# Cross attention's values product: four full-precision products a head become twelve on high and low parts

## The reference, cut to what matters

```
kv = mem @ mem_w_kv                      # once; 256 x 2048
mem_k, mem_v = split into 4 heads of 256
for each of the 2 layers:
    ...
    q = (x @ wq)                          # 256 x 1024, 4 heads of 256
    s = q @ mem_k.T / 16                  # each head, 256 x 256
    p = softmax(s)
    o = p @ mem_v                         # each head, 256 x 256: the changed product
    x = layer_norm(ALPHA * x + o @ wo)
    x = layer_norm(ALPHA * x + mlp(x))
```

## Time and profile before

| | |
|---|---|
| median of 3 runs | 953.45 us (952.93 to 953.58) |
| profiled execution, first to last instruction | 1903.2 us |
| PE busy in it | 1896.1 us |
| DVE busy | 710.1 us |
| ACT busy | 520.2 us |
| granted TensorE clock in it | 1.000 |

### The profile page before, as it was taken

One profiled execution on the slowest core, in us unless ns is written; L12 is line 12 of the kernel. 1 busy time (PEld: TensorE's weight loads), 2 busy tenths in 40 slices (PEclk: granted clock), 3 DMA queues, 4 the chain that ended last, 5 costly groups with the idle time before them and its releaser, 6 DMA issues.

```text
span 1903.2 us, 13114 instructions
## 1 busy us (share of the span) xinstructions
PE 1896.1 (100%) x5108; PEld 1373.0 (72%) x5108; DVE 710.1 (37%) x963; ACT 520.2 (27%) x732; POOL 60.6 (3%) x96
## 2 busy tenths in 40 slices
PE   9999999999999999999999999999999999999998
PEld 9669766766777776767666777667887667777766
DVE  6323234425343332443343343334334442232232
ACT  4233221313222223122132222232233232222221
POOL 0000000000000001000000000001000000000010
DMA  7332142215434433032154344341310243223200
GB/s 261 132 103 74 66 143 89 74 59 176 146 133 137 150 133 111 1 145 76 50 174 151 133 144 137 129 147 50 111 67 22 89 136 96 89 89 110 89 22 22
DMA packets 109660, 203.00 MB, mean 107 GB/s; under 512 B 4332, under 2 KB 75264, under 8 KB 106272
## 3 DMA queue, kind: packets, MB, share of 16 engines
q1 hardware_dynamic: 106000, 189.15, 29.7%
q0 software_dynamic: 3168, 12.24, 1.8%
q10 hardware_dynamic: 432, 0.79, 0.1%
HBM read 201.09 MB, written 1.06 MB: 106 GB/s over the span
## 4 chain that ended last, share of the span: by engine, by line
PE 99%; issue 0%; ACT 0%; DVE 0%; POOLq 0%; POOL 0%; ACTq 0%
PE WB L377 20%; PE YB L402 12%; PE YB L395 12%; PE YB L410 12%; PE WB L380 10%; PE YB L463 6%; PE WB L395 3%; PE WB L410 3%; PE WB L402 3%; PE WB L359 2%; PE WB L366 2%; PE WB L362 2%; PE YB L879 2%; PE WB L745 2%; PE WB L501 1%; PE YB L852 1%
## 5 line engine op out<-in xcount | busy, mean ns | idle before, releaser
L1801 DVE TENSOR_TENSOR wl<-raw,wh 128x2048 fp32r<-128x2048 f32 x144 | 331.5, 2306 | 283.4 <-ACT wh L1161 279.5
L377 PE MATMUL WB<-XS,wh 128*128 128x512 f32 x832 | 410.8, 675 | 0.0
L377 PEld LDWEIGHTS WB<-XS,wh 128*128 128x128 f32 x832 | 245.3, 303 | 118.0 <-issue 107.4
L1161 ACT CAST wh<-raw 128x2048 fp32r<-128x2048 f32 (+1 forms) x147 | 278.6, 1898 | 156.7 <-PE YB L410 84.3
L380 PEld LDWEIGHTS WB<-XS,wl 128*128 128x128 f32 x832 | 211.3, 317 | 35.3 <-issue 32.4
L380 PE MATMUL WB<-XS,wl 128*128 128x256 f32 x832 | 215.9, 440 | 0.0
L402 PE MATMUL YB<-wl,FHT 128*128 128x512 f32 x344 | 196.5, 676 | 0.0
L410 PE MATMUL YB<-wh,FLT 128*128 128x512 f32 x344 | 196.3, 674 | 0.0
L395 PE MATMUL YB<-wh,FHT 128*128 128x512 f32 x344 | 196.2, 673 | 0.0
L1343 ACT COPY U<-WB 128x256 f32<-128x256 f32 x102 | 33.0, 375 | 411.9 <-PE WB L380 411.9
L410 PEld LDWEIGHTS YB<-wh,FLT 128*128 128x128 f32 x344 | 103.1, 300 | 57.5 <-issue 49.5
(11 more groups left out here) (373 smaller groups left out, 1803.2 us busy)
## 6 DMA issues: line engine op xcount, KB each, us to landing
raw<-in_mlp_w SPq DMA_DIRECT2D x64, 1024.0 KB, 5.2
raw<-in_w_ada_t SPq DMA_DIRECT2D x24, 1024.0 KB, 4.8
raw<-in_mlstm_w_in SPq DMA_DIRECT2D x11, 1024.0 KB, 5.3
raw<-in_w_ffn_down SPq DMA_DIRECT2D x11, 1024.0 KB, 4.8
raw<-in_w_ffn_gate SPq DMA_DIRECT2D x10, 1024.0 KB, 5.4
raw<-in_w_ffn_up SPq DMA_DIRECT2D x10, 1024.0 KB, 5.3
raw<-in_mem_w_kv SPq DMA_DIRECT2D x8, 1024.0 KB, 5.1
raw<-in_xattn_wq SPq DMA_DIRECT2D x8, 1024.0 KB, 5.1
```

The source lines that it names most:

```text
L377: e.matmul(W[:, :], H[:, at(k)], XS[:, k, :], start=k == 0, stop=False)
L1161: f = e.copy(w[:, 0:a * b], raw[:, 0:a * b])
L1801: f = e.tensor_tensor(L[:, 0:a * b], raw[:, 0:a * b], H[:, 0:a * b].bitcast(F32), ALU.subtract)
```

## The change

The values product becomes three fp32r products on high and low parts, as everywhere else in the kernel. `VM` is replaced by `VMH` and `VML`, `PT` by `PTH` and `PTL`. They lie in one tensor of type fp32r named `LAT`, which now spans the same memory as `AR`; so rows of the change name them `LAT`. ACT's copies stay where they were and now write the high parts. DVE gets twelve new subtractions of 512 columns from a bank: `value_low(j)` (two for each panel) and `turned_low(h)` (one a head and layer). The banks of the panels and of the transposed probabilities are now freed by these DVE subtractions, not by ACT's copies. To make room, the two rows of the second layer's first norm (`BV[2]`, `BV[3]`) and the mixer's `V1` lie elsewhere, and the second of these rows is loaded later, once DVE has done the last hidden block of the first MLP.

```diff
-        VM = AR[:, 2048:4096].rearrange("p (t c) -> p t c", t=2)
+        VMH, VML = (LAT[:, a:a + 2048].rearrange("p (j t c) -> p t j c", j=2, t=2) for a in (2048, 4096))
-        PT = TMP[:, 2048:2560]
+        PTH, PTL = LAT[:, 8192:8704], LAT[:, 6144:6656]
...
                 def values(h):
                     W = bank(("xv", i, h))
-                    e.wait_ge(*act_mlstm["mv", 1, 1])
+                    e.wait_ge(*dve_mlstm["mv", 1, 1])
                     e.wait_ge(*act_xa["pt", i, h])
+                    def product(d, v, x, m, start=False, stop=False):
+                        c = 256 * (h % 2) + 128 * d
+                        return e.matmul(W[:, 256 * d:256 * d + 256], v[:, m, h // 2, c:c + 128],
+                                        x[:, 256 * m:256 * m + 256], start=start, stop=stop)
                     for d in range(2):
                         for m in range(2):
-                            p = e.matmul(W[:, 256 * d:256 * d + 256],
-                                         VM[:, m, 256 * h + 128 * d:256 * h + 128 * d + 128],
-                                         PT[:, 256 * m:256 * m + 256], start=m == 0, stop=m == 1)
+                            product(d, VMH, PTH, m, start=m == 0)
+                        for m in range(2):
+                            product(d, VML, PTH, m)
+                        e.wait_ge(*dve_xa["pt", i, h])
+                        for m in range(2):
+                            p = product(d, VMH, PTL, m, stop=m == 1)
...
                     e.wait_ge(*pe_mlstm["mv", j, t])
-                    e.copy(VM[:, t, 512 * j:512 * j + 512], W[:, :]).then_inc(act_mlstm.add(("mv", j, t)))
-                    freed["mv", j, t] = act_mlstm["mv", j, t]
+                    e.copy(VMH[:, t, j, :], W[:, :]).then_inc(act_mlstm.add(("mv", j, t)))
...
-                    e.copy(PT, W[:, :]).then_inc(act_xa.add(("pt", i, h)))
-                    freed["xt", i, h] = act_xa["pt", i, h]
+                    e.copy(PTH, W[:, :]).then_inc(act_xa.add(("pt", i, h)))
...
+            def value_low(j):
+                for t in range(2):
+                    W = bank_of.get(("mv", j, t), WB[0])
+                    e.wait_ge(*act_mlstm["mv", j, t])
+                    e.tensor_tensor(VML[:, t, j, :], W[:, :], VMH[:, t, j, :].bitcast(F32), ALU.subtract
+                                    ).then_inc(dve_mlstm.add(("mv", j, t)))
+                    freed["mv", j, t] = dve_mlstm["mv", j, t]
...
             lo_to(M["mv", 0, 1] + 3)
+            value_low(0)
             head_c(3)
...
             lo_to(M["mv", 1, 1] + 3)
+            value_low(1)
...
+                def turned_low(h):
+                    W = bank_of.get(("xt", i, h), WB[0])
+                    e.wait_ge(*act_xa["pt", i, h])
+                    if h > 0:
+                        e.wait_ge(*pe_xa["v", i, h - 1])
+                    e.tensor_tensor(PTL, W[:, :], PTH.bitcast(F32), ALU.subtract).then_inc(dve_xa.add(("pt", i, h)))
+                    freed["xt", i, h] = dve_xa["pt", i, h]
...
-                scores(1)
-                scores(2, lambda: query_low(3))
+                scores(1, lambda: turned_low(0))
+                def amid():
+                    query_low(3)
+                    turned_low(1)
+                scores(2, amid)
                 values(0)
                 scores(3)
                 q(3)
                 values(1)
+                turned_low(2)
                 lo_to(M["wo", i, 0] + 3)
                 values(2)
+                turned_low(3)
...
+            e.wait_ge(*dve_mlp["h", 0, 15])
+            e.dma_start(BV[3], I["ln_b"][1, 0].partition_broadcast(128)).then_inc(d_ln10, 16)
```

More of the change, by code:

```diff
@@ L193, in build_program @@
         FLT = sb("FLT", [128, 1280], F32R)
-        with nc.sbuf_tensor("LAT", [128, 6144], F32R) as LAT:
+        with nc.sbuf_tensor("LAT", [128, 8800], F32R) as LAT:
             pass
@@ L200, in build_program @@
         FL = [FLT[:, 512 * i:512 * i + 512] for i in range(2)]
-        BV = [sb(f"bv{i}", [128, 1024]) for i in range(2)] + [AR[:, 4096:5120], AR[:, 5120:6144]]
+        BV = [sb(f"bv{i}", [128, 1024]) for i in range(2)] + [AR[:, 1024:2048], AR[:, 6144:7168]]
         IDN = sb("IDN", [128, 128])
@@ L227, in build_program @@
         QC = AR[:, 2080:2080 + 2048].rearrange("p (k c) -> p k c", k=8)
-        V1 = AR[:, 4128:4128 + 2064].rearrange("p (t h c) -> p t h c", t=2, h=4)
+        V1 = AR[:, 4128:4128 + 2064].rearrange("p (h t c) -> p t h c", t=2, h=4)
         OG = AR[:, 6192:6192 + 2048].rearrange("p (t c) -> p t c", t=2)
@@ L2714, in gpsimd @@
             e.dma_start(CROW, c_row.partition_broadcast(128)).then_inc(d_crow, 16)
-            for n, x, src in ((2, "g", I["ln_g"]), (3, "b", I["ln_b"])):
-                e.dma_start(BV[n], src[1, 0].partition_broadcast(128)).then_inc(d_ln10, 16)
-                bv_of[x, "10"] = n, (d_ln10, 32)
+            e.dma_start(BV[2], I["ln_g"][1, 0].partition_broadcast(128)).then_inc(d_ln10, 16)
+            bv_of["g", "10"] = 2, (d_ln10, 32)
+            bv_of["b", "10"] = 3, (d_ln10, 32)
             layer_norm(0, 0)
```

## The result

The changed kernel takes 957.84 us (median of 5, 956.8 to 958.29) against 953.58 for the kernel before beside it (952.93 to 953.93): a ratio of 1.0041, 95% interval 1.003 to 1.0052. It is 4.3 us slower.

What follows compares the result with a forecast made beforehand. PE was taken to bound the kernel, busy 1896.1 of 1903.2 us profiled, at half those intervals when timed. 953.45 + 4.1 (bank wait) - 2.5 (attention, three heads of four) = 955.0 us, range 950.8 to 957.8.

Steps and rivals of the forecast that it cites:

- likeliest case: Whole kernel: the prediction's main account, 955.0 us, with its own range 954.0 to 956.0 and chance 0.45.
- the sum: Whole kernel: +4.1 for the panel's bank less 2.5 in attention, +1.6 on 953.45, giving 955.0 us.
- PE idles nowhere else anew: Changed kernel's profile: besides the 1.8 us wait at panel 1's first product, PE shows no new idleness.
- PE's pace: Whole kernel: PE alone is slow in the trace; timed runs have its intervals halved, DVE, ACT and POOL unchanged.
- The bank: Ahead of panel 1: PE waits for DVE to free panel 0's banks, 4.1 us timed, 1.8 in the trace.
- Nothing downstream gives it back: Behind panel 1: ACT, DVE and the loads all shift along, so the 4.1 us wait stays lost.
- The clock: Rival, at the pause before panel 1: PE's pace also drops, 4 us of work costing 2; 957.0 us, chance 0.15.
- The price of a values product: Cross attention: twelve products replace the plain ones, saving 0.85 us a head in the trace, 0.42 timed.
- values(0) gains nothing: Cross attention, head 0: PE already waits 0.6 us for query_low(3), 1.0 with the shorter product, so no gain.
- Attention gains nothing: Rival, cross attention: DVE's subtractions also arrive late for values(1) to (3); 957.6 us, chance 0.12.
- All scales: Rival, whole kernel: handovers stay as in the trace, wait 0.9 and gain 3.4 us; 950.9 us, chance 0.15.
- All of 3.4 is gained: Rival, cross attention: no wait for query_low(3) exists, so 3.4 us are gained; 954.2 us, chance 0.13.

Runs made afterwards that it cites:

- second trace of before: The kernel before, unchanged, profiled a second time: 953.36 us, with 951.7 us of span.
- late_filled: late_bank with 34 added products of 256 columns on PE ahead of panel 1: 957.94 us, ratio 1.0046.
- late_bank: The kernel before with only two added DVE subtractions, behind the low part of wout 0, freeing panel 0's banks: 959.16 us, ratio 1.0064.
- earliest: The change with value_low(0) moved ahead of the low parts of mv (1, 1) and wout 0 on DVE: 951.43 us, ratio 0.9976.
- swapped: earliest with turned_low(1) ahead of query_low(3) in DVE's order, in both layers: 954.06 us, ratio 1.0004.
- filled: The change with 34 added products of 256 columns on PE between y_turn(0) and panel 1: 955.57 us, ratio 1.0022.
- low_first: The change with value_low(0) moved ahead of the low part of wout 0 on DVE: 952.87 us, ratio 0.9991.
- half_low: The change with the low part of wout 0 cut in two on DVE and value_low(0) between the halves: 956.22 us.

## Why the prediction was right, and where its terms were off

The main mechanisms were right and the time was at the edge: 957.84 lies at the top of the range, 950.8 to 957.8 (4.3 us on 953.45 would be 957.7), and outside the likeliest case's own 954.0 to 956.0. The step that came short is the sum: it left the clock at nothing. The signs named for the profile, a wait of 1.8 us and a span of 1898, couldn't be looked for, since the change's trace was not slow; "PE idles nowhere else anew" held but for 0.2 us (192.07, below). In the chances, slower adds up to 0.42 and same to 0.43; the text has them the other way round.

**PE's pace (the step on which all rested): right.** The second trace of before has PE at about half of the first one's intervals and DVE unchanged (0.227 us for 0.459, and 2.29 for 2.29).

**The bank: the right wait, 0.5 too small.** 4.1 predicted; panel 1 starts 4.6 us later than without the wait, 4.35 of it idleness. The chain was as read: ACT's last copy, its high part of `wout` 0, DVE's low part, two subtractions, 5.9 us from that copy's start (117.36, the second of the two in the row of 116.89) against 6.08 from the earlier trace rows. What was off is PE's arrival, 1.99 predicted after that start and 1.4 in fact (116.71, plus the 2.10 that lie between 117.40 and 119.50 in the second trace of before). At full pace PE is done with panel 0 while ACT still makes a high part (115.09 to 116.98), so the copies start late. The first trace didn't have this. The net cost timed by late_filled, without the clock, is 4.2 us: near 4.1, because the next point took back as much as this one missed.

**"Nothing downstream gives it back": wrong by 0.6.** In the second trace of before, ACT waited for the load of a `wq` chunk, and the first norm came late by that:

```profile
143.86 1.91 ACT L1161 CAST wh<-raw 128x2048 fp32r<-128x2048 f32 x1 [3.28 <-DMA raw<-in_xattn_wq]
145.80 1.62 DVE L1809 TENSOR_TENSOR wl<-raw,wh 128x1408 fp32r<-128x1408 f32 x1 [2.90 <-ACT wh L1161]
...
152.54 0.66 PE L501 MATMUL WB<-IDN,X 128*128 128x128 f32 x4 [0.56 <-DVE X L2072]
```

In the change's trace the load has the pause's time to land and PE doesn't idle there; 0.6 us come back. The same holds in every trace in which panel 1 starts late, 0.6 to 0.7 us each. Late_bank and late_filled are among them, and have nothing else of the change. Of the two changed kernels in which it doesn't start late, earliest has the wait (0.89 us) and swapped has not, so it varies there from run to run.

**The clock: the term left out of the sum.** It stood among the rivals with 0.15 and a price of 2; it happened, with 2.1 to 2.3 us by filled and 2.4 in the traces. That is most of what lies between 955.0 and 957.84. The likeliest case was wrong to leave it out: a pause of 4 us on an engine that otherwise never idles for one was the very case on which the first trace was silent.

**The price of a values product: 0.42 a head predicted, 0.29 measured.** Halving the first trace's intervals was too simple: half of them is 1.86 and 1.43 us. The second trace of before has

```profile
183.80 1.89 PE L745 MATMUL WB<-AR 128*128 128x256 f32 x8
...
185.53 0.60 PE L735 MATMUL WB<-IDN,AR 128*128 128x128 f32 x4
...
187.11 0.47 ACT L1376 ACTIVATE AR<-WB,SM 128x256 f32<-128x256 f32 x1
...
187.73 1.99 PE L745 MATMUL WB<-AR 128*128 128x256 f32 x8
```

1.73 us for the plain products, and the change's

```profile
189.49 1.60 PE L746 MATMUL WB<-LAT 128*128 128x256 f32 x12
...
190.93 0.60 PE L735 MATMUL WB<-IDN,AR 128*128 128x128 f32 x4
191.29 0.48 PE L721 MATMUL WB<-KHL,FHT 128*128 128x256 f32 x2
191.33 0.69 DVE L2171 TENSOR_TENSOR FLT<-U,FHT 128x512 fp32r<-128x512 f32 x1
191.61 0.40 PE L723 MATMUL WB<-KHL,FHT 128*128 128x256 f32 x2
...
192.07 0.50 PE L726 MATMUL WB<-KHL,FLT 128*128 128x256 f32 x2
...
192.51 0.48 ACT L1384 ACTIVATE AR<-WB,SM 128x256 f32<-128x256 f32 x1
...
193.13 1.71 PE L746 MATMUL WB<-LAT 128*128 128x256 f32 x12
```

1.44 for the twelve: the float32 products were overpriced by 0.13, and the others were right. 8 x 0.29 = 2.3 at most.

**"values(0) gains nothing": wrong.** query_low(3) ends at 192.02, 4.2 after the maximum of head 1 (187.82), not 5.0, and PE waits for it some 0.2 us only (192.07 against the 191.85 at which two products of 0.12 from 191.61 end). I had taken the 3.36 us from maximum to scaled probabilities out of the earlier trace rows as DVE's and ACT's own. But in the first trace ACT's exponentials stood behind its copy of head 0, which waited for PE; at full pace the copy comes earlier and the chain takes 2.8. Part of a chain that I took as unshrinkable was waiting for PE. The 0.2 us of waiting are not lost either. From values(0) to values(1) it is 3.93 us before (183.80 to 187.73) and 3.64 with the change (189.49 to 193.13), 0.29 less. In both, values(1) takes the bank of head 2's scores, and so starts 0.15 us after ACT's last exponential of head 2 has read it (187.58 and 192.99); those exponentials stand behind ACT's copy of turned(1), which comes sooner when values(0) is shorter. The count had no such wait. The two errors, of price and of heads, cancel by luck: 6 x 0.42 predicted, 8 x 0.29 possible; 2.2 in the traces, 2.3 timed by earliest, 2.5 on record.

**The rivals.** "Attention gains nothing" gives 957.6, closer to the measured time than my own case, and is refuted by earliest. "All scales" is refuted by the second trace. "All of 3.4 is gained" was right that all eight products gain and had the same price too high. The time came out of the clock's rival, 957.0 on record.

**The sum as measured:** 4.2 (bank less what comes back, late_filled) + 2.1 (clock, filled) - 2.3 (attention and all else, earliest) = 4.0; measured 4.3. Each is a difference of medians, and those of the kernel before alone lie between 953.43 and 953.72.

## What to carry to other kernels

When the reader of a bank changes engines, the bank's release moves to the end of that engine's queue at that place. Look at what stands ahead of the new reader there, and put the release first where it can go: here two lines of order made the same change 2.3 us faster instead of 4.3 slower.

Compare the span of a profiled execution with the timed one before reading idle times. Where one engine ran slow, redo each handover with its intervals shortened, and take care that a chain on other engines doesn't itself contain a wait for the slow one.

A pause of some microseconds on TensorE can cost its clock on top; price it, and if it can't be removed, work in it may cost less than idleness.

## What the runs showed of the hardware

The granted clock of the first trace stands at 1.000 although products of 512 columns came every 0.459 us on average, where four took 0.91 us in the second trace, 0.227 each. A clock column alone did not tell that PE was slow. In the change's trace, at 0.50 granted, such products start 0.43 us apart, close to the first trace's pace; so that one may have run at the 1.2 GHz level all along without a record of it. That is not shown, and why PE was slow is open.

At full pace a plain float32 product of 256 columns took 2 x 0.216 us and an fp32r one 0.120, a ratio of 3.6. In the first trace the starts are 2 x 0.443 and 0.223 apart, a ratio of 4.0. The fp32r product did not gain the full factor of two.

With the same pause of 4.6 us from one product's start to the next, the clock was at the 1.2 GHz level for 6.8 us in the change's trace (the windows shown above give 2 x (0.16 x 4 + 0.47 x 6) = 6.9) and for 3.4 in late_bank's (2 x 0.28 x 6). Narrower windows, two of the change and then two of late_bank, tell when it fell:

```profile
119.00:121.70 2.70, 0.05 (x1) 0.00 (x0) 2.21 (x2) 0.77 (x1) 0.00 (x0) 1.00 0.39 93
121.80:123.30 1.50, 0.00 (x0) 0.00 (x0) 1.50 (x4) 0.00 (x0) 0.00 (x0) 0.50 1.01 418
```

```profile
124.00:124.90 0.90, 0.88 (x4) 0.78 (x5) 0.43 (x3) 0.37 (x1) 0.00 (x0) 1.00 1.00 300
125.00:128.40 3.40, 3.40 (x9) 2.63 (x8) 0.99 (x4) 1.09 (x7) 1.19 (x5) 0.50 0.65 249
```

In the change it fell while PE was idle; in late_bank it fell at 125, when PE had been at work again since 124.02. With 1.9 us (low_first) it stayed up, and with 3.6 us (half_low) it stayed up in the traced run and by the times and mean clocks most likely fell in others. The Trainium skill (TensorE: Matmul & The Clock Gate, Part 1) says that idleness lowers the clock and sustained work restores it. By that rule the traces of the change and of late_bank agree in that a pause was followed by the low level and work by the high one; in late_bank the fall came after the pause, not in it.
